# A decoder trunk on one core: the zeros for the expert buffers stored in 28 pieces during the dense layer

## What is computed

```python
h = h + mla(rms_norm(h, attn_norm[0]), ...)
h = h + (silu(hn @ w_gate) * (hn @ w_up)) @ w_down          # hn = rms_norm(h, ffn_norm[0])
h = h + multiscale_pool(rms_norm(h, attn_norm[1]), ...)
h = h + moe_swiglu(rms_norm(h, ffn_norm[1]), ...)            # top 2 of 8, gates by softmax
return rms_norm(h, final_norm)
```

## Time and profile before

| | |
|---|---|
| median of 3 runs | 1179.94 us (1179.6 to 1181.88) |
| profiled execution | 1184.12 us, its span 1182.5 us |
| TensorE busy | 1103.1 us, 93% of the span |
| VectorE, ScalarE, GpSimd busy | 385.7, 278.1, 57.1 us |
| DMA moved | 225.26 MB, of them 36.32 MB by GpSimd's queue |

### The profile page before, as it was taken

One profiled execution on the slowest core, in us unless ns is written; L12 is line 12 of the kernel. 1 busy time (PEld: TensorE's weight loads), 2 busy tenths in 40 slices (PEclk: granted clock), 3 DMA queues, 4 the chain that ended last, 5 costly groups with the idle time before them and its releaser, 6 DMA issues.

```text
span 1182.5 us, 19051 instructions
## 1 busy us (share of the span) xinstructions
PE 1103.1 (93%) x7414; PEld 1002.0 (85%) x7414; DVE 385.7 (33%) x703; ACT 278.1 (24%) x533; POOL 57.1 (5%) x99
## 2 busy tenths in 40 slices
PE   5999999799999999999997899999999999999980
PEld 4878877688888888888786799999999999999980
DVE  5586672354244442453564001010101010101015
ACT  5445552242224222232340001010101010101011
POOL 2210110000000000000002000000000000000002
PEclk9999999899999999999998999999999999999995
DMA  7027758434415144151203999999999999999996
GB/s 254 17 91 196 215 150 206 130 116 134 107 54 141 52 126 106 53 142 53 71 19 138 285 274 270 272 266 301 267 303 280 304 283 305 281 298 286 301 237 232
DMA packets 273230, 225.26 MB, mean 190 GB/s; under 512 B 29968, under 2 KB 246032, under 8 KB 273200
## 3 DMA queue, kind: packets, MB, share of 16 engines
q1 hardware_dynamic: 260192, 185.88, 56.2%
q0 software_dynamic: 11616, 36.32, 10.8%
q10 hardware_dynamic: 1392, 2.64, 0.6%
HBM read 198.43 MB, written 26.35 MB: 190 GB/s over the span
## 4 chain that ended last, share of the span: by engine, by line
PE 86%; DVE 6%; DMA 5%; ACT 1%; issue 1%; POOL 0%; DVEq 0%; SPq 0%; ACTq 0%; POOLq 0%
PE bank L1303 26%; PE bank L1317 14%; PE bank L905 13%; PE bank L907 13%; PE bank L906 13%; DMA scratch<-in_ffn_norm 2%; PE bank L1077 1%; PE bank L1364 1%; DMA stage_own<-in_moe_w_up 1%; PE bank L917 1%; PE bank L1281 1%; PE bank L1207 1%; PE bank L1057 1%; PE bank L1068 1%; PE bank L1292 1%
## 5 line engine op out<-in xcount | busy, mean ns | idle before, releaser
L1303 PE MATMUL bank<-scratch,stage_own 128*128 128x128 f32 (+1 forms) x2720 | 327.5, 278 | 8.4 <-DMA stage_own<-in_moe_w_gate 3.0
L1303 PEld LDWEIGHTS bank<-scratch,stage_own 128*128 128x128 f32 x2720 | 318.2, 191 | 10.5 <-DMA stage_own<-in_moe_w_gate 3.4
L1821 DVE TENSOR_TENSOR qr_now<-krT,bank 128x128 f32<-128x128 f32 (+1 forms) x80 | 23.4, 292 | 378.1 <-ACT krT L855 378.1
L1317 PE MATMUL bank<-qr_now,stage_own 128*128 128x128 f32 (+1 forms) x1152 | 143.5, 278 | 0.0
L1317 PEld LDWEIGHTS bank<-qr_now,stage_own 128*128 128x128 f32 x1152 | 137.3, 192 | 0.0
L905 PE MATMUL bank<-big_hi,w_lo 128*128 128x512 f32 (+2 forms) x352 | 134.4, 382 | 0.0
L907 PE MATMUL bank<-big_hi,w_hi 128*128 128x512 f32 (+2 forms) x352 | 134.3, 381 | 0.0
L906 PE MATMUL bank<-big_lo,w_hi 128*128 128x512 f32 (+2 forms) x352 | 134.2, 381 | 0.0
L855 ACT ACTIVATE krT<-bank 128x128 f32<-128x128 f32 (+1 forms) x80 | 22.5, 281 | 376.9 <-PE bank L1303 376.9
L1390 DVE TENSOR_TENSOR w_lo<-stage_own,w_hi 128x1024 fp32r<-128x1024 f32 (+1 forms) x91 | 105.4, 1203 | 14.0 <-ACT w_hi L608 13.9
L608 ACT CAST w_hi<-stage_own 128x1024 fp32r<-128x1024 f32 (+1 forms) x91 | 88.9, 1032 | 15.0 <-DMA stage_own<-in_mla_w_down 6.5
(11 more groups left out here) (243 smaller groups left out, 1146.5 us busy)
## 6 DMA issues: line engine op xcount, KB each, us to landing
stage_own<-in_moe_w_gate SPq DMA_DIRECT2D x82, 512.0 KB, 5.9
stage_own<-in_moe_w_up SPq DMA_DIRECT2D x82, 512.0 KB, 6.3
stage_own<-in_moe_w_down SPq DMA_DIRECT2D x72, 512.0 KB, 4.6
stage_own<-in_ffn_w_gate SPq DMA_DIRECT2D x21, 512.0 KB, 5.7
stage_own<-in_ffn_w_up SPq DMA_DIRECT2D x21, 512.0 KB, 6.9
stage_own<-in_ffn_w_down SPq DMA_DIRECT2D x21, 512.0 KB, 3.6
xbuf<-zeros POOLq DMA_DIRECT2D x2, 5184.0 KB, 41.9
scratch<-xbuf POOLq DMA_DIRECT2D x9, 576.0 KB, 6.3
```

The costliest lines, as they stand in the source:

```text
L1303: last = t_.matmul(dst[:, 0:n], w[:, k * P:(k + 1) * P], xT[:, k, 0:n], start=k == 0, stop=k == KD - 1)
L1317: last = t_.matmul(bank[4 + k // 3][:, col:col + n], w[0:parts, k * P:(k + 1) * P], e_act[0:parts, par, 0:n], start=first and k % 3 == 0, ...
L1821: v.tensor_tensor(e_act[:, par, 0:n], e_silu[:, par, 0:n], bank[2 * par + 1][:, 0:n], ALU.mult).then_inc(prod_ready, 1)
```

## The change

The zeros now come from the first row tile of `xn` in SBUF (`zero_rows`, 128 partitions of 4 KB), which GpSimd clears once the transposes of the dense layer's norm are done. They are stored in 28 pieces: 21 for `xbuf`, XZERO = 124 rows each, one row from each of 124 partitions, and 7 for `ybuf`, YZERO = 166 rows each, two rows from each of 83 partitions. In every iteration of the dense layer GpSimd issues two x pieces once VectorE's product of the second hidden tile is there, then an x and a y piece once VectorE has added the first half's four row tiles. `xbuf` grows from 2592 to 2604 rows. ScalarE waits for all 28 pieces before the norm that follows the dense layer, since this norm writes the tile that they read; the scatter's wait is raised to 28 x 16.

```diff
-XROWS = (JMAX + 2) * C
+XZERO = -(-(JMAX + 2) * C // (FI * FG))
+XROWS = FI * FG * XZERO
+YZERO = 2 * -(-(JMAX - E) * C // (2 * FI))
...
+        zero_rows = scratch[:, 0:D]
...
+        zeros_ready = sem("zeros_ready")
...
-            pool.wait_ge(weight_lo, plan.unit("pair", 1, 1) + 1)
-            half = (JMAX + 2) // 2 * C
-            for rows in (xbuf[0:half, :], xbuf[half:, :], ybuf[E * C:, :]):
-                pool.dma_start(rows.rearrange("(p r) (c n) -> p (r c) n", p=ZP, n=P),
-                               zeros[0:ZP, :].unsqueeze(1).broadcast_to([ZP, rows.shape[0] // ZP * (D // P), P])
-                               ).then_inc(zero_stored, 16)
...
+            pool.wait_ge(xnT_done, 2 * T)
+            g.memset(zero_rows, 0.0).then_inc(zeros_ready, 1)
+            pool.wait_ge(zeros_ready, 1)
+            for i in range(FI):
+                for j in range(FG):
+                    if j == 0:
+                        pool.wait_ge(prod_ready, i * FG + 2)
+                    elif j == 2:
+                        pool.wait_ge(h_ffn, i * 8 + 4)
+                    at = (i * FG + j) * XZERO
+                    pool.dma_start(xbuf[at:at + XZERO, :], zero_rows[0:XZERO, :]).then_inc(zero_stored, 16)
+                at = (JMAX * C - FI * YZERO) + i * YZERO
+                pool.dma_start(ybuf[at:at + YZERO, :].rearrange("(p r) n -> p r n", r=2),
+                               zero_rows[0:YZERO // 2, :].unsqueeze(1).broadcast_to([YZERO // 2, 2, D])).then_inc(zero_stored, 16)
             pool.wait_ge(xn_ready, 3 * T)
...
-            pool.wait_ge(zero_stored, 48)
+            pool.wait_ge(zero_stored, 16 * 4 * FI)
...
+            act.wait_ge(zero_stored, 16 * 4 * FI)
             for t in range(T):
                 act.wait_ge(h_ffn, 8 * (FI - 1) + 4 + t + 1)
                 norm_std(2 * T + t, t)
```

## The result

The changed kernel takes 1196.19 us (median of 4 runs, 1195.16 to 1197.76), the kernel before, on the same chip, 1180.76 us: ratio 1.0132, 95% interval 1.0114 to 1.0149, slower by 15.4 us. The profiled execution took 1196.28 us with a span of 1194.7 us, 12.2 us more than before; that of before lay 4 us above its median, so the medians are the fairer pair.

The account below looks back on a forecast made before the run. The prediction took TensorE as the bound, with 86% of the chain that ends last. Adding 30.7 us and removing 13.7 gave +17.0 on 1179.94, so 1197 us, with a range from 1164 to 1206.

Parts of the forecast that it names:

- Terms 1 to 4: Attention and dense layer's start: TensorE's stops and slow-clock work caused by the old zero stores go, 13.7 us together.
- the second stop: Before the dense layer: TensorE's 5.98 us wait for normed rows goes, with slow-clock work of 1.8 and 1.1 us.
- term 4: In the attention: TensorE's 2.2 us wait for VectorE's scaling, slow while GpSimd issues the third zero store, goes.
- Term 5: In the dense layer: GpSimd's memset and 28 issues of about 0.6 us beside a busy TensorE add 0.
- Term 6: In the dense layer: 15.4 MB of zero stores over seven iterations hides if it spreads over all 16 engines.
- Term 7: At the dense layer's end: ScalarE waits for the last y piece, on one DMA engine; +30.7 us.
- The 1.2 us for the clock: After TensorE's long stop at the dense layer's end: slow-clock work costs 1.2 us more.
- The first rival: At the dense layer's end: pieces spread over many engines, land by 586.4 us, only savings remain, 1166 us; chance 0.30.
- Weights late: In the dense iterations: the y piece's one engine also delays gate and up weights, 1258 us; chance 0.04.
- no relief: Before the dense layer: SyncE's ten loads, not the zeros, hold the gain; only 2.2 us regained, 1208 us; chance 0.03.

## Why the prediction was right

It gave 1197 us for 1196.19, and the mechanism that decides is the one that was foreseen. That the numbers meet within 1 us is in part luck. The working had 17.0 us more than before; the medians differ by 15.4 us, the two profiled spans, on which it was made, by 12.2. Point by point:

- **Terms 1 to 4, gone: 13.7 us.** The trace shows 13.9 us up to the layer's last matmul. The gain landed in 7.0 us (allowed: 7.8), x was there, the slow matmuls and the scaling of 3.50 us are gone. That the gain was held mainly by its queue and not by the bandwidth is shown by the run with that load on ScalarE's queue (11.5 us). The split among the four terms was not measured one by one, save the 7.9 us of that run for the terms of the second stop, which I had at 6.0 + 1.8 + 1.1 = 8.9, and term 4, where 0.25 us of TensorE's wait is left of 2.2 without the third store.
- **Term 5, GpSimd's own work.** Cost nothing, but a y issue takes 2.5 us, not 0.6 to 0.7: an issue with the repeated row took 2.54, 1.56 and 0.70 us for one, two and fourteen engines.
- **Term 6, the traffic hides.** Right for TensorE, which has no stop in the iterations; the median landing of the gate tiles there rose from 5.6 to 8.9 us. With 84 partitions it is 5.9, so most of the rise came with the y pieces' one engine.
- **Term 7, one engine for 83 partitions.** Right, and it decided. I had 35.5 us from issue to landing, it took 34.4. The parts differ: I had added 0.032 us to 0.166 for every small packet in between, 32.9 us; a pair took 0.179, which makes 29.7 us. With the 2.6 us fixed that leaves 2.1 us, about what the issue took longer than that of an x piece (2.54 against 0.52 us); that it is the issue is not shown. TensorE's stop grew by 28.8 us where I had 29.5. The 1.2 us for the clock hardly came: the first 64 matmuls behind the stop took 9.75 us, and 9.57 before.
- **Left out:** what is gained behind the stop, 2.7 us, as much as TensorE's waits for the experts' weights fell. It is the largest part of the 4.8 us between the 17.0 forecast and the 12.2 of the spans; the rest is the clock (1.2), a stop shorter by 0.7 us and 0.2 us more gained before it.
- **The first rival, pieces that spread.** Half of it is true. The plain x pieces spread, for 31 packets of 0.16 us on each of four engines, with 2.6 us fixed, would be 7.6 us, and they land in 5.5; the packet counts fit sixteen engines with eight rows each and would be 368 more for every piece on four. Four is what the rule gives that I used, from the Trainium skill, "DMA: Bandwidth & Descriptors", section on why a DMA increments its semaphore by 16; the exception which the same section names holds here for them and for plain copies of 83 rows, and not for the form with the repeated row. The rival's price was too low: with 84 partitions the last piece landed 9.0 us after its issue, not 5.9 (8.4 us is the median of all seven, each with weight loads beside it), and TensorE waited 5.54 us before the pooling layer in place of 2.26. 1170.65 us, not 1166.
- **Weights late** and **no relief** did not come. But the first came to the large stores, when those were moved into the layer.

What I had not seen is the gain load behind the last y piece. I wrote that its own wait ends later; true while ScalarE waits for the pieces, and hidden by that wait. Only the run that removed it showed it.

## What to carry over

Before cutting a transfer into pieces, look at the number of rows and the form of each piece: 84 for 83 partitions, or two plain copies for one with a repeated row, made some 27 us of difference here (15.4 us slower than before in place of 12.0 us faster, each on its own chip). Read a late small load first by what stands ahead of it in its own queue; another queue may be the whole remedy. Background traffic beside loads that TensorE depends on did no harm in pieces of 496 and 672 KB spread over the layer; as one block of large stores it stopped TensorE for 6 and 12 us, and the average share of DMA time didn't tell that.

## What was not expected of the hardware

- By the packet counts, engines that carry no data of a GpSimd copy still handle a tiny packet for each packet of a busy engine: 28304 packets with 83 partitions, 11056 with 84.
- GpSimd's issue time of a y piece grows with the load of the busiest engine: 0.70, 1.56 and 2.54 us for 12, 86 and 166 packets on it. Another form has another price: the old x stores, 108 packets on each of twelve engines, took 4.27 us.
- The same 83 rows are spread as a plain copy and go through one engine with a row repeated by a stride of zero: 7.5 against about 32 us.
- Beside a long store of GpSimd's, SyncE's issue of one load lasted 22.18 us against 0.37.
